# Gated part of the first layer: next head's scores and decay rows issued ahead of this head's weighted sums

## What is computed

```python
def step(carry, xs):
    c_st, n_st, m_st = carry
    qc, kc, vc, ic, fc = xs
    b = jnp.cumsum(fc, axis=-1)
    log_d = jnp.where(tri, b[..., :, None] - b[..., None, :] + ic[..., None, :], -jnp.inf)
    inter = b + m_st[..., None]
    m_t = jnp.maximum(inter, jnp.max(log_d, axis=-1))
    s = jnp.einsum('bhtd,bhsd->bhts', qc, kc) * jnp.exp(log_d - m_t[..., None])
    w_inter = jnp.exp(inter - m_t)
    num = (jnp.einsum('bhts,bhsv->bhtv', s, vc)
           + w_inter[..., None] * jnp.einsum('bhvd,bhtd->bhtv', c_st, qc))
    den = jnp.sum(s, axis=-1) + w_inter * jnp.einsum('bhd,bhtd->bht', n_st, qc)
    h = num / jnp.maximum(jnp.abs(den), jnp.exp(-m_t))[..., None]
...
```

## Time and profile before

| | us |
|---|---|
| median of 3 runs | 4538.23 |
| lowest and highest run | 4534.09, 4547.59 |
| the profiled execution | 4546.98 |
| its span, first to last instruction | 4544.9 |
| PE busy | 3724.0 (82%) |
| DVE busy | 2778.7 (61%) |
| ACT busy | 1617.0 (36%) |
| POOL busy | 1400.9 (31%) |
| mean granted TensorE clock | 0.948 |

### The profile page before, as it was taken

How to read it: one execution, slowest core, us unless ns; L and a number is a source line. 1 busy time by engine, 2 the same in 40 slices (tenths; PEclk the granted TensorE clock), 3 DMA queues, 4 the chain that set the end, 5 groups by cost and what they waited for, 6 DMA issues and landing times.

```text
span 4544.9 us, 39811 instructions
## 1 busy us (share of the span) xinstructions
PE 3724.0 (82%) x10606; PEld 1685.3 (37%) x10606; DVE 2778.7 (61%) x6903; ACT 1617.0 (36%) x4735; POOL 1400.9 (31%) x1337
## 2 busy tenths in 40 slices
PE   5987988878898777797887777979877768897776
PEld 2444543224443222255432223444422224442222
DVE  2227566787666766455667765347667753776775
ACT  0123144444444444142444442114444430444443
POOL 0000244444444444101444442004434420444442
PEclk7988999999999999998999999989999989999999
DMA  5334599999999999744999998529999982999997
GB/s 226 144 134 187 224 421 422 421 421 410 417 419 422 412 421 415 318 159 171 422 421 420 417 421 346 185 113 422 421 421 417 417 345 86 418 421 421 421 413 316
DMA packets 207346, 1573.57 MB, mean 346 GB/s; under 512 B 23088, under 2 KB 23216, under 8 KB 30352
## 3 DMA queue, kind: packets, MB, share of 16 engines
q0 software_dynamic: 191952, 1370.57, 73.0%
q1 hardware_dynamic: 14976, 200.26, 11.3%
q10 hardware_dynamic: 192, 0.20, 0.0%
HBM read 1569.69 MB, written 1.25 MB: 346 GB/s over the span
## 4 chain that ended last, share of the span: by engine, by line
DMA 48%; PE 26%; DVE 9%; ACT 5%; issue 3%; DVEq 1%; POOL 1%; ACTq 0%; POOLq 0%
DMA arena<-uv,idx 47%; PE banks L863 11%; PE banks L489 6%; DVE arena L1771 4%; PE banks L836 3%; ACT diag L1121 1%; PE banks L522 1%; DMA weight_ring<-weights 1%; ACT wgt L1119 1%; POOL arena L436 1%; ACT gel L1117 1%; PE banks L677 1%; ACT L1096 1%; PE banks L697 1%; ACT L1117 1%
## 5 line engine op out<-in xcount | busy, mean ns | idle before, releaser
L863 PE MATMUL banks<-arena,diag 128*128 128x512 f32 x5120 | 2519.8, 629 | 586.8 <-ACT diag L1121 584.6
L1771 DVE CUSTOM_DVE_ANT_0 arena<-arena 128x1024 f32<-128x1024 f32 x1280 | 1568.3, 1225 | 941.7 <-DMA arena<-uv,idx 934.7
L436 POOL DMA_INDIRECT arena<-uv,idx x1280 | 1371.8, 1072 | 1998.8 <-PE banks L863 1772.0
L863 PEld LDWEIGHTS banks<-arena,diag 128*128 128x128 f32 x5120 | 935.3, 196 | 2114.0 <-ACT diag L1121 1303.2
L1117 ACT ACTIVATE gel<-dot 128x1 f32<-128x1 f32 x1280 | 258.3, 202 | 1658.0 <-DVE dot L1771 1657.0
L1121 ACT ACTIVATE diag<-consts_sb,wgt 128x128 f32<-128x128 f32 x1280 | 514.0, 402 | 92.4 <-issue 5.4
L1119 ACT ACTIVATE wgt<-gel,gate 128x1 f32<-128x1 f32 x1280 | 376.8, 294 | 90.7 <-issue 3.5
L836 PE MATMUL banks<-arena,weight_ring 128*128 128x256 f32 x1280 | 291.8, 383 | 4.4 <-DVE arena L1274 4.4
L419 POOL DMA_DIRECT2D row_ring<-mods x34 | 18.2, 540 | 837.2 <-DMA mods<-diag 258.5
L836 PEld LDWEIGHTS banks<-arena,weight_ring 128*128 128x128 f32 x1280 | 245.3, 192 | 63.0 <-issue 30.6
L489 PE MATMUL banks<-weight_ring,arena 128*128 128x512 f32 (+1 forms) x620 | 262.8, 583 | 1.9 <-DVE arena L1274 1.1
(11 more groups left out here) (241 smaller groups left out, 2291.4 us busy)
## 6 DMA issues: line engine op xcount, KB each, us to landing
weight_ring<-weights SPq DMA_DIRECT2D x77, 2048.0 KB, 8.7
arena<-weights SPq DMA_DIRECT2D x10, 2048.0 KB, 9.0
arena<-uv,idx POOLq DMA_INDIRECT x1280, 15.2
row_ring<-mods POOLq DMA_DIRECT2D x34, 512.0 KB, 10.2
row_ring<-gains POOLq DMA_DIRECT2D x18, 512.0 KB, 6.6
arena<-keys SPq DMA_DIRECT2D x4, 1024.0 KB, 4.8
arena<-weights SPq DMA_DIRECT2D x2, 1536.0 KB, 7.6
arena<-weights SPq DMA_DIRECT2D x3, 1024.0 KB, 5.2
```

The source lines that it names most:

```text
L436: pool.indirect_dma_start(out=ring[:, k % SLOTS, :], out_offset=None, in_=A[f"uv{l}"], in_offset=bass.IndirectOffsetOnAxis(ap=idx[:, UNIT_ ...
L863: ins = mm_(bank[:, yb, :], diag[:, k % SLOTS, :], ring[:, k % SLOTS, D + hf * 512:D + hf * 512 + 512], start=first, stop=last, skip_group ...
L1771: sig(V.tensor_tensor_reduce(out=ring[:, s, 0:D], in0=ring[:, s, 0:D], in1=xnat_of(u[0], u[1]), scale=1.0, scalar=0.0, op0=ALU.mult, op1=A ...
```

## The change

PE issues `A` and `M` of head `h+1` ahead of head `h`'s conditioning products and weighted sums. DVE adds the first mask of head `h+1` right behind `WT(h,1)`, ahead of the four normalisations of head `h`. ACT's program, the buffers, the number of banks and the products themselves stay.

```diff
--- before.py
+++ after.py
@@ -592,7 +592,8 @@
                     pe.wait_ge(*after("qkT", 3))
                     pe.wait_ge(*after("vml_ones"))
                     pe.wait_ge(*after("ev", 0, "v", 3, 0))
-                    for h in range(4):
+
+                    def scores_and_decay(h):
                         o = 64 * (h % 2)
                         for s in range(4):
                             b = new_bank(0, "A", h, s)
@@ -602,6 +603,11 @@
                             b = new_bank(0, "M", h, d)
                             mm_(bank[:, b, :], selr[:, h, :], mrow[:, d, :], start=True, stop=True)\
                                 .then_inc(sems["pe"], done("pe", ("mm", 0, "M", h, d)))
+
+                    scores_and_decay(0)
+                    for h in range(4):
+                        if h < 3:
+                            scores_and_decay(h + 1)
                         for d in range(2):
                             wt = v3(EW1 if d else EW0, 4, TOK)
                             if d == 0:
@@ -1393,7 +1399,8 @@
                     for h in range(4):
                         for d in range(2):
                             wt = v3(EW1 if d else EW0, 4, TOK)
-                            masked(h, d)
+                            if h == 0 or d:
+                                masked(h, d)
                             for s in range(4):
                                 dve.wait_ge(*after("ev", 0, "A", h, s))
                             dve.wait_ge(*after("E", h, d))
@@ -1402,6 +1409,8 @@
                                     ins = V.tensor_tensor(wt[:, s, t0 * P:t1 * P], wt[:, s, t0 * P:t1 * P],
                                                           ats[:, s, t0 * P:t1 * P], ALU.mult)
                             sig(ins, ("WT", h, d))
+                        if h < 3:
+                            masked(h + 1, 0)
                         for d in range(2):
                             for tp in range(2):
                                 b = b_(0, "N", h, d, tp)
```

## The result

The kernel after takes 4557.4 us, median of 16 runs (4550.69 to 4562.25). The kernel before, run 16 times in the same comparison, takes 4545.9 (4534.09 to 4553.31); the median of the three shown ahead of the prediction, 4538.23, was 7.7 us lower. The ratio is 1.003, with a 95% interval of 1.0023 to 1.0037: slower by 0.3%. The two medians are 11.5 us apart, which is 0.25%. The forecast was +1.5 us.

What follows compares the result with a forecast made beforehand. No engine is full; a chain passing between PE, ACT and DVE bounds the gated part. -2.4 (first transition) + 0.6 (banks) + 3.3 (clock) = +1.5 us on 4538.23 gives 4539.7, said as 4540; range 4530 to 4551.

Steps and rivals of the forecast that it cites:

- The banks: PE's third score product of heads 2 and 3 waits 5.6 us for M(h,1)'s bank; the two transitions lose 0.4 to 0.8 us.
- The early mask: DVE's mask for the next head, moved ahead of the normalisations: gains nothing, waiting for M(2) too, and holds no normalisation up.
- 7.2 us from weights to weights: DVE's chain after a head's normalisations, weights, mask, exponentials, weights, ending at the next T(h): 7.2 us.
- The clock: One PE clock fall of 1.64 us behind the new hole in each of the two later transitions: 3.3 us lost.
- The first transition: Transition from head 0 to 1: PE's half clock ends about 301.6, T(1) comes at 321.0 instead of 323.4, gaining 2.4 us.
- T(1): T(h) is the end of head h's last weight product; T(1) was forecast at 321.0 us.
- The slower rival: Half clock from the third A to the last N in both later transitions: 10.2 us each, 4561 us in all; 5%.
- point of decision: The slower rival turns the result to "slower" from about 7.5 us per transition, half clock over three quarters of the chain.
- The ceiling: If nothing held PE back, DVE's own chain of 13.85 us a head against 17.73: 11.6 us for three transitions.
- The scale: Whole-kernel time: 1.5 us on the 4538.23 median, said as 4540; no change below about 0.3%, 13.6 us, can be told.
- The signs: Profile checks; wrong if the hole is under 2 us, head 3's last normalisation shifts over 6, or time moves more elsewhere.

Runs made afterwards that it cites:

- run 16: Not a label: the text says "run 16 times"; the kernel before, unchanged, was run 16 times in the same comparison and takes 4545.9 us.

## Why the prediction was wrong

- **The banks.** Right. The hole was forecast as 5.6 us before the third score product of heads 2 and 3, and is 5.43 and 5.81. That it comes from the ring of seven, the dealing of the banks alone has shown. Both transitions were expected at 17.9 to 18.1 us at full clock; with the hole filled by whole-array products one took 18.14.
- **The early mask.** Right that it holds no normalisation up: it waits 3.76 us for PE, and the normalisation behind it waits 5.72 more. "The early mask gains nothing" was wrong. Without it a transition takes 3.5 us longer. The sum had that gain in it all the same, since its 7.2 us from weights to weights leave no time for a first mask and its exponentials behind the normalisations.
- **The clock, the step that failed.** "I put one such fall, 1.64 us, into each of the two transitions", and its reason, "because the half clock that followed that hole was over before the next N took its 2.50 us again". The clock fell inside the hole and was at its half from the scores to the end of the conditioning products: 3.71 + 3.70 + 3.57, 11 us from 321.08 to 332.06, for 5.6 us of work. That is 5.4 us per transition in place of 1.64, 7.5 us too little in two. The row that I took the size from was one in which PE ran sums. What now stands behind the hole is scores and decay products, and the runs show that these leave a low clock low (28 us of them with extra scores ahead of head 1).
- **The first transition.** The same error. "The clock is at its half until about 301.6" was read off a stage in which the conditioning products and then sums stood there. With scores and decay products in their place it stayed low until shortly before the conditioning products ended at 309.0. T(1) - T(0) was 19.46 and not 15.3, 4.1 us. With the 7.5 this is 11.6 of the 12 us by which the stage missed its forecast. A slip in the same sum changed nothing: it took its tail of 0.3 us against 0.86 us for one of four `A`, and 3.63 / 4 is 0.91.
- **The slower rival** named the mechanism and priced it at 10.2 us per transition, since it kept the sums at half clock too. They ran at full speed, so it was 5.4. Its point of decision, 7.5 us per transition, was wrong as well: it counted on the gain of 2.4 us in the first transition, which went by the same cause. With the 1.7 us lost there in its place it comes to 5.6. Its own sum did allow up to 4.6 us more for that transition; 4.1 were measured. I gave it 5% where the rows bore about as much for it as against it.
- **The ceiling** was sized rightly and declared out of reach, since I took the ring and the order as given. Another order of the same products on the same ring reaches 13.6 to 14 us a transition.
- **The scale.** The forecast went by a median of 4538.23 of three runs. The same kernel's median over 16 is 4545.9. The range, 4530 to 4551, was built on the lower figure. It took both errors to put the result outside: 11.5 us on top of 4538.23 would have been 4549.7, inside it, though the clock step would have been as wrong. That "a measurement of this kernel tells no change below about 0.3%, 13.6 us" was wrong too: with 16 runs of each the interval is 0.07% to either side.
- **The signs.** The prediction called itself wrong if the last normalisation of head 3 ended over 6 us from where it had ended. With T(3) 11.4 us later, that sign came.

## What to carry to other kernels

Issuing work ahead lengthens the time that its results occupy banks: follow the ring one full turn in the new order and ask which read-out each product will wait for, since on an engine that runs in order everything behind it waits too. When a hole or a block of products moves, the duration rows of the old place no longer hold: price what follows at either level of the clock, and put products that raise the clock again between those that don't. Two small edits tell the causes apart: a filler product takes away the hole and leaves the blocked bank, another dealing of the banks takes away both.

## What the runs showed of the hardware

At every rise of the granted clock inside this stage, in all thirteen kernels, PE was running or had just run conditioning products, sums or whole-array products, all of 128 rows, and never only scores (64 rows) or decay products (4 rows). With scores and decay products alone the clock stayed at 1.2 GHz through 28 us of unbroken work. They do not pull it down at once: six repeated scores ran at full speed in 5.31 us. Behind scores and decay products the clock also fell under a busy PE, as within the conditioning products at 343.56 of the kernel with the hole filled by whole-array products (3.29 us instead of 1.92). That rows are what matters, and not the data or the number of instructions, is not shown. With PE busy throughout, the same eight score instructions took 7.19 us behind decay products and 3.70 behind conditioning products. The Trainium skill (TensorE: Matmul & The Clock Gate, section "HAM oscillation — how this bites in real kernels") puts the throttled clock down to waits of PE; that agrees with the fall inside the holes of 5.4 and 5.8 us, and explains neither the stretches that stayed low nor the falls under a busy PE.
